# Stationary tiles of four output stages at other offsets from the weights

## The reference

```python
def _swiglu(x, w_in, w_out):                 # w_out: 2816 x 1024; twice, "f1" and "f2"
    g, u = jnp.split(x @ w_in, 2, axis=-1)
    return (jax.nn.silu(g) * u) @ w_out

def recurrent_mixer(...):                    # "a"
    ...
    return jnp.einsum('bsc,cd->bsd', y * jax.nn.silu(gate), w_out)   # 1536 x 1024

def shortconv_mixer(...):                    # "b"
    ...
    return jnp.einsum('bsc,cd->bsd', y * jax.nn.silu(gate), w_out)   # 1536 x 1024
```

## Time and profile before

| | |
|---|---|
| median of three runs | 890.83 us |
| span of the profiled execution | 887.0 us |
| TensorE busy (matmul) | 879.6 us, 99% |
| VectorE busy | 625.0 us, 70% |
| ScalarE busy | 489.4 us, 55% |
| GpSimd busy | 64.4 us, 7% |
| HBM read | 167.05 MB, 190 GB/s over the span |

### The profile page before, as it was taken

One profiled execution on the slowest core, in us unless ns is written; L12 is line 12 of the kernel. 1 busy time (PEld: TensorE's weight loads), 2 busy tenths in 40 slices (PEclk: granted clock), 3 DMA queues, 4 the chain that ended last, 5 costly groups with the idle time before them and its releaser, 6 DMA issues.

```text
span 887.0 us, 11473 instructions
## 1 busy us (share of the span) xinstructions
PE 879.6 (99%) x4628; PEld 752.3 (85%) x4628; DVE 625.0 (70%) x808; ACT 489.4 (55%) x661; POOL 64.4 (7%) x89
## 2 busy tenths in 40 slices
PE   9999999999999999999999999999999999999997
PEld 7888888888888888888888888888999888888886
DVE  6887776467767656577577777446979857888872
ACT  6865564445444556446565555435887644555551
POOL 2000000003021110000000000000390000000000
PEclk9999999999999999999999999999999999999999
DMA  9955555455753444455655555546534456555521
GB/s 352 368 188 191 191 189 199 147 190 179 282 198 127 180 168 173 184 190 190 237 190 190 191 190 190 189 182 251 184 106 181 151 187 254 190 190 191 190 95 48
DMA packets 26948, 169.89 MB, mean 192 GB/s; under 512 B 3616, under 2 KB 3664, under 8 KB 7952
## 3 DMA queue, kind: packets, MB, share of 16 engines
q1 hardware_dynamic: 24368, 161.23, 50.3%
q0 software_dynamic: 2240, 7.66, 2.5%
q10 hardware_dynamic: 288, 0.27, 0.1%
HBM read 167.05 MB, written 1.05 MB: 190 GB/s over the span
## 4 chain that ended last, share of the span: by engine, by line
PE 97%; DVE 1%; ACT 1%; issue 0%; ACTq 0%
PE acc L1839 15%; PE acc L1642 15%; PE acc L1640 15%; PE acc L1641 15%; PE acc L2101 8%; PE acc L1841 7%; PE acc L2103 4%; PE acc L1655 2%; PE acc L1883 2%; PE acc L2053 2%; PE acc L2054 2%; PE acc L2052 2%; PE aux L2037 1%; PE aux L1764 1%; PE acc L1885 1%; PE aux L1641 1%
## 5 line engine op out<-in xcount | busy, mean ns | idle before, releaser
L996 DVE TENSOR_TENSOR w_lo<-raw,w_hi 128x2048 fp32r<-128x2048 f32 x147 | 336.8, 2300 | 89.9 <-ACT w_hi L522 89.5
L522 ACT ACTIVATE w_hi<-raw 128x2048 fp32r<-128x2048 f32 x145 | 275.7, 1911 | 62.6 <-DMA raw<-weights 62.4
L1839 PE MATMUL acc<-xT,w_hi 128*128 128x512 f32 x576 | 200.4, 394 | 0.0
L1841 PE MATMUL acc<-xT,w_lo 128*128 128x256 f32 x576 | 159.7, 277 | 0.0
L1839 PEld LDWEIGHTS acc<-xT,w_hi 128*128 128x128 f32 x576 | 108.0, 188 | 25.0
L1640 PE MATMUL acc<-w_hi,xT 128*128 128x512 f32 x312 | 124.0, 398 | 0.0
L1642 PE MATMUL acc<-w_hi,xT 128*128 128x512 f32 x312 | 121.8, 390 | 0.0
L1641 PE MATMUL acc<-w_lo,xT 128*128 128x512 f32 x312 | 121.5, 390 | 0.0
L2101 PE MATMUL acc<-xT,w_hi 128*128 128x512 f32 x320 | 111.3, 394 | 0.0
L1841 PEld LDWEIGHTS acc<-xT,w_lo 128*128 128x128 f32 x576 | 108.2, 188 | 0.0
L2103 PE MATMUL acc<-xT,w_lo 128*128 128x256 f32 x320 | 88.7, 277 | 0.0
(11 more groups left out here) (263 smaller groups left out, 1290.4 us busy)
## 6 DMA issues: line engine op xcount, KB each, us to landing
raw<-weights SPq DMA_DIRECT2D x147, 1024.0 KB, 4.8
gain_pre<-gains POOLq DMA_DIRECT2D x5, 512.0 KB, 5.0
raw<-weights SPq DMA_DIRECT2D x4, 512.0 KB, 7.5
gain_post<-gains POOLq DMA_DIRECT2D x3, 512.0 KB, 5.6
gate_w<-gate_w_in POOLq DMA_DIRECT2D x1, 1536.0 KB, 8.5
x_turned<-x_turned_in SPq DMA_DIRECT2D x4, 256.0 KB, 4.9
x<-x_in SPq DMA_DIRECT2D x2, 512.0 KB, 11.6
bias_raw<-bias_in POOLq DMA_DIRECT2D x16, 64.0 KB, 3.2
```

Of the source, the lines that this page charges most:

```text
L522: a.activation(w_hi[:, g % RING], raw[:, g % RING], ACT.Copy).then_inc(hi_done, 1)
L996: v.tensor_tensor(w_lo[:, slot], raw[:, slot], w_hi[:, slot].bitcast(F32), ALU.subtract)\
L1839: m.matmul(dst, w_hi[:, slot, w], xT[:, k].rearrange("p a q -> p (a q)"), start=k == 0, stop=False)
L1841: i = m.matmul(dst[:, 0:S], w_lo[:, slot, w], xT[:, k, 0], start=False, stop=k == KD - 1)
```

## The change

The high and low tiles of `f1_out`, `f2_out`, `a_out` and `b_out` become tensors of their own that begin some words behind a multiple of 256 bytes: `shifted` allocates a row that is `words` longer and hands out the view behind these words. High parts are at 4, 56, 40 and 24 words, low parts at 60, 1, 52 and 2 words: 16, 224, 160, 96 and 240, 4, 208, 8 bytes. The low part of the `hT` tiles moves up by a further 256 bytes to make room, and the tensors around them by 512; `yg_4` moves by 192 bytes and `squares` to `area` + 36864. The functions that write or read the tiles take the one of their stage. No instruction, wait or transfer is added, taken away or moved in the order.

```diff
-        hT_hi = at("hT_hi", [P, FF // P, S], F32R, area)
-        hT_lo = at("hT_lo", [P, FF // P, S], F32R, area + 22528)
-        silu_g = at("silu_g", [P, T, 256], F32, area + 45056)
-        prod = at("prod", [P, 2, T, 256], F32, area + 47104)
-        gate_c = at("gate_c", [P, 2, S], F32, area + 51200)
-        prod_c = at("prod_c", [P, 2, S], F32, area + 53248)
+        def shifted(name, chunks, place, words):
+
+            return at(name, [P, chunks * S + words], F32R, place)[:, words:].rearrange("p (c q) -> p c q", q=S)
+
+        hidden_hi_of = {"f1": shifted("hT_hi_f1", FF // P, area, 4), "f2": shifted("hT_hi_f2", FF // P, area, 56)}
+        hidden_lo_of = {"f1": shifted("hT_lo_f1", FF // P, area + 22784, 60),
+                        "f2": shifted("hT_lo_f2", FF // P, area + 22784, 1)}
+        silu_g = at("silu_g", [P, T, 256], F32, area + 45568)
+        prod = at("prod", [P, 2, T, 256], F32, area + 47616)
+        gate_c = at("gate_c", [P, 2, S], F32, area + 51712)
+        prod_c = at("prod_c", [P, 2, S], F32, area + 53760)
...
-        yg_4 = at("yg_4", [P, 2, 512], F32, area + 63488)
+        yg_4 = at("yg_4", [P, 2, 512], F32, area + 63488 + 192)
         yg = [yg_0[:, n] for n in range(4)] + [yg_4[:, n] for n in range(2)]
-        yT_hi = at("yT_hi", [P, CH, S], F32R, area + 51200)
-        yT_lo = at("yT_lo", [P, CH, S], F32R, area + 12288)
-
-        x_scaled = at("x_scaled", [P, 2, DM // 2], F32, area + 24576)
-        squares = at("squares", [P, 2, DM // 2], F32, area + 28672)
+        yT_hi_a = shifted("yT_hi_a", CH, area + 51200, 40)
+        yT_lo_a = shifted("yT_lo_a", CH, area + 12288, 52)
+        yT_hi_b = shifted("yT_hi_b", CH, area + 51200, 24)
+        yT_lo_b = shifted("yT_lo_b", CH, area + 12288, 2)
+
+        x_scaled = at("x_scaled", [P, 2, DM // 2], F32, area + 24576 + 512)
+        squares = at("squares", [P, 2, DM // 2], F32, area + 36864)
...
-            out_stage("a_out", yT_hi, yT_lo, CH, lambda n: pe.wait_ge(y_low, n + 1), lambda: None, 4,
+            out_stage("a_out", yT_hi_a, yT_lo_a, CH, lambda n: pe.wait_ge(y_low, n + 1), lambda: None, 4,
                       free=lambda t: pe.wait_ge(pair_taken, 6 + 2 * t))
```

More of the change, by code:

```diff
@@ L650, in hidden_hi @@
                 def hidden_hi(j, par):
+                    hT_hi = hidden_hi_of[which]
                     act.wait_ge(bank_full, f0 + 1 + j)
@@ L676, in chunk_round @@
                     act.wait_ge(prod_ready, c_before + n + 1)
-                    a.activation(hT_hi[:, STRAIGHT + n, :], prod_c[:, n % 2], ACT.Copy).then_inc(chunk_hi, 1)
+                    a.activation(hidden_hi_of[which][:, STRAIGHT + n, :], prod_c[:, n % 2], ACT.Copy).then_inc(chunk_hi, 1)
                 if g0 == 0:
@@ L837, in gated_hi @@
                 act.wait_ge(yg_ready, n + 1)
-                a.activation(yT_hi[:, 2 * n:2 * n + 2, :], yg[n].rearrange("p (c q) -> p c q", c=2), ACT.Copy)\
+                a.activation(yT_hi_a[:, 2 * n:2 * n + 2, :], yg[n].rearrange("p (c q) -> p c q", c=2), ACT.Copy)\
                     .then_inc(bank_hi, 1)
@@ L926, in b_hi @@
                 act.wait_ge(b_y_ready, 1 + j)
-                dst = yT_hi[:, j, :] if isinstance(j, int) else yT_hi[:, bass.ds(j, 1), :].rearrange("p a q -> p (a q)")
+                dst = yT_hi_b[:, j, :] if isinstance(j, int) else yT_hi_b[:, bass.ds(j, 1), :].rearrange("p a q -> p (a q)")
                 a.activation(dst, b_y[:, par], ACT.Copy).then_inc(bank_hi, 1)
@@ L1142, in swiglu @@
                 g0, f0, q0 = FIRST_GROUP[st], FIRST_FILL[st], FIRST_SPLIT[st]
+                hT_hi, hT_lo = hidden_hi_of[which], hidden_lo_of[which]
                 gate0 = {"f1": 0, "f2": GATES_F2}[which]
@@ L1449, in gated_lo @@
                 dve.wait_ge(bank_hi, FIRST_SPLIT["gate"] + n + 1)
-                v.tensor_tensor(yT_lo[:, 2 * n:2 * n + 2].rearrange("p c q -> p (c q)"), yg[n],
-                                yT_hi[:, 2 * n:2 * n + 2].rearrange("p c q -> p (c q)").bitcast(F32), ALU.subtract)\
+                v.tensor_tensor(yT_lo_a[:, 2 * n:2 * n + 2].rearrange("p c q -> p (c q)"), yg[n],
+                                yT_hi_a[:, 2 * n:2 * n + 2].rearrange("p c q -> p (c q)").bitcast(F32), ALU.subtract)\
                     .then_inc(y_low, 1)
@@ L1534, in b_lo @@
                 one = (slice(j, j + 1) if isinstance(j, int) else bass.ds(j, 1))
-                v.tensor_tensor(yT_lo[:, one, :].rearrange("p a q -> p (a q)"), b_y[:, par],
-                                yT_hi[:, one, :].rearrange("p a q -> p (a q)").bitcast(F32), ALU.subtract)\
+                v.tensor_tensor(yT_lo_b[:, one, :].rearrange("p a q -> p (a q)"), b_y[:, par],
+                                yT_hi_b[:, one, :].rearrange("p a q -> p (a q)").bitcast(F32), ALU.subtract)\
                     .then_inc(bank_free, 1)
@@ L1858, in wait_chunk @@
                         pe.wait_ge(chunk_lo, c_before + 2 * g - STRAIGHT + 2)
-                out_stage(f"{which}_out", hT_hi, hT_lo, FF // P, wait_chunk, lambda: None, n + 1, 4,
+                out_stage(f"{which}_out", hidden_hi_of[which], hidden_lo_of[which], FF // P, wait_chunk, lambda: None, n + 1, 4,
                           lambda t: pe.wait_ge(up_summed, c_before + CHUNKS - 1 + t))
@@ L2111, in _ @@
                     b_transposes(1, 1)
-            out_stage("b_out", yT_hi, yT_lo, CH, lambda n: pe.wait_ge(bank_free, f0 + 2 * n + 2),
+            out_stage("b_out", yT_hi_b, yT_lo_b, CH, lambda n: pe.wait_ge(bank_free, f0 + 2 * n + 2),
                       free=lambda t: pe.wait_ge(b_summed, B_PAIRS - 1 + t))
```

## The result

The changed kernel takes 893.75 us (median of four runs) against 889.83 us for the kernel before (four runs, one more than above): a ratio of 1.0047, interval 1.0032 to 1.0062, so 2.8 to 5.5 us slower. The profiled execution has a span of 891.8 us against 887.0.

The account below looks back on a forecast made before the run. TensorE, busy 99% of the 887.0 us span, was taken as the bound, by matmul spacing alone. 272 triples x 20 ns = 5.4 us, all else nothing: 890.8 + 5.4 = 896.3 us, range 885 to 907.

Parts of the forecast that it names:

- The row it rested on: In na_out, low tiles 32 bytes off the 256-byte grid: 700 ns a triple against 680 in ret_out, taken as the offset's price.
- step 1: In the four output stages, 272 triples (three matmuls in turn) lose the grid: 20 ns each, 5.4 us slower.
- the forecast alone: Output stages cost 10 to 30 ns more a triple, 893.5 to 899 us; chance 0.36.
- steps 2 and 3: ScalarE and VectorE writes of the tiles at new places, and moved scratch tensors with yg_4 and squares: cost nothing.
- The dearer rival: In the output stages each load off the grid pays for itself: 30 to 60 ns a triple, 899 to 907 us; chance 0.27.
- no effect: The change does nothing TensorE sees, or gains and losses among the stages cancel: 890.8 us; chance 0.17.
- The faster rival: Load and weight stream collide on the common grid; another distance frees up to 10.4 ns a matmul, 882.3 us; chance 0.20.

Follow-up runs that it names:

- e5_na_on_grid: Kernel before with temp_at moved down by 32 bytes, so na_out's low part lies at 0 modulo 256 from the weights; single run 888.86 us.
- e6_all_by_32: Kernel before with the start of all tensors moved up by 32 bytes, those at temp_at staying; ratio 0.9997.
- e8_by_256: Changed kernel with the four stages' parts at 0 or 256 bytes instead of their odd offsets; ratio 0.9988 to the kernel before.
- e1_low_only: Changed kernel with the high parts of the four stages back at 0, low parts at the change's offsets; ratio 1.0031 to the kernel before.
- e2_high_only: Changed kernel with the low parts of the four stages back at 0, high parts at the change's offsets; ratio 1.0040 to the kernel before.
- e4_coarse: Changed kernel with one part of each stage at 64 (f1_out, f2_out) or 128 bytes (a_out, b_out), the other at 0; ratio 1.0033 to the kernel before.

## Why the prediction was right

- **Bound.** TensorE's spacing alone set the time, and nothing took over: the idle time before the slower groups is 0.0, and the span grew by 4.8 us where the four stages grew by 4.7.
- **The row it rested on.** That the 20 ns of `na_out` come from the 32 bytes was an inference from two stages; `e5_na_on_grid` and `e6_all_by_32` show it.
- **The price, step 1.** Taken: +20 ns for a triple, 5.4 us. Measured: 18, 20, 20 and 13 ns, 4.9 us by the interiors, and +3.9 us by the medians (2.8 to 5.5). The term that was clearly too large is `b_out`'s (13, at 96/8); `f1_out`'s was off by 2 ns. The choice not to add up three loads is borne out by the two kernels with one part each. The reason I gave, that in `na_out` the third matmul was left alone, did not hold: I expected two of the three lines of the `hT` stages to slow, and all three did. So the single price was in part luck, and so was its size: the parts tried alone cost between 0 and 20 ns, and one row, at 32 bytes, could not have told that the four pairs of the change would all be dear ones.
- **The time.** Forecast 896.3 us, measured 893.75, which is at the low edge of the 893.5 to 899 of the forecast alone. Of the 2.5 us between them 1.5 are the price (5.4 against 3.9 by the medians) and 1.0 the starting value, 890.8 where four runs have 889.83. The span is nearer, 892.4 forecast and 891.8 measured. That span and median lie 3.8 us apart, "which stays", was misread: in the runs with both numbers the time is 1.7 or 1.8 us over the span of the same execution, and the profiled execution of before was one of its quicker ones. The sum did not use this gap, so nothing hangs on it; but it is most of why the spans differ by 4.8 us and the medians by 3.9.
- **Writes and scratch, steps 2 and 3.** Nothing, as said. The low parts of the `hT` stages, at 240 and 4 bytes, are still written in 424 to 428 ns a piece of 256 columns (424 to 426 before), and `e8_by_256`, with all the moved scratch, is not slower.
- **The dearer rival** (each load pays) is refuted by `e1_low_only` and `e2_high_only`, **no effect** by every stage. What was said for the latter about fp32 transposes does stand: in `e5_na_on_grid`, where `tmp` is at 0 modulo 256 from the weights, four of them still take 0.45 us.
- **The faster rival** didn't come about: of the offsets tried, with each part alone or together, none gave a 512-column triple under 680 ns. But my reason against it, that 13.3 ns may be what a load simply needs, is not shown either: the 256-column triples of `a_in` lost 5 of their 40 ns of surplus when the ring was moved.
- **Two read ports.** The matmul's price changes by up to 3% with the distance between its two operands, on the same instructions, waits and transfers; between stages there are up to some 7 ns a triple more that the offsets modulo 256 don't explain. The Trainium skill, page TensorE: Matmul & The Clock Gate, section "Step-by-step: what each phase is for", says that TensorE has two independent SBUF read ports, and that loading the next tile takes nothing from the running matmul. The runs do not bear out the second part for these fp32r matmuls (680 against 700 ns a triple).
- **Lines of 16 bytes.** The Trainium skill, page SBUF — State Buffer, section "Specifications (TRN2)", says that the memory has lines of 16 bytes, with a penalty for each step to a new line. Worked out from that alone, a start 16 or 64 bytes off would be as good as one at 0; the runs have 20 ns for 16 bytes (`e2_high_only`) and 13 for 64 (`e4_coarse`).

## What to carry to other kernels

In a stream of 512-column fp32r matmuls that each load a new stationary tile, start every stationary tile a multiple of 256 bytes from the moving operand. A tensor placed from the other end of the memory easily breaks this, and mostly costs 2 to 3% of its stage without any idle time in the profile. For 256 columns this is not a rule: in `a_in` a distance of 32 bytes was the faster one. To see it, divide the length of a stretch by the matmuls in it and compare stages that run the same code; busy share and waits show nothing.

## What the runs showed of the hardware

- A triple of 128x512 fp32r matmuls takes 680 ns at a granted clock of 1.00 with the two operands a multiple of 256 bytes apart, and 690 to 700 at most other distances: 4, 8, 16, 32, 64, 96, 128, 160, 192, 208 and 224 bytes were tried for at least one part; the mildest of these was the high part at 192, 687 ns.
- The prices of the high and the low part do not add up: together they cost 18, 20, 20 and 13 ns, where the low parts alone cost 0, 20, 17 and 13 and the high parts alone 20, 20, 13 and 10.
- The price depends on the distance and not on the address: 32 bytes for the weights alone cost 16 us of span, 32 bytes for all tensors from `base` on none (887.3 against 887.0).
- Open: why the low part at 240, and either part at 252, cost nothing while the low part at 248 and the high part at 240 do; why one pair has 700 ns in one stage and 693 in another (the place modulo 512 is untested); and why the 256-column triples of `a_in` are faster at 32 bytes (355 against 360 ns). That the load and the stream get in each other's way in the memory would fit a dependence on distance alone, but no run shows such a meeting.
